# The row exchange of the rotary turns in the second network's query projections: as SBUF to SBUF transfers instead of as products

## The chip, the cores and the metric

The kernel runs on one core of one Trainium2 chip. The metric is the time of one execution in microseconds (us). Before the change it is 2290.31 us, the median of 3 runs (2289.16 to 2290.59).

A core has five engines that matter here: TensorE (PE in the rows, with its weight loads as PEld), VectorE (DVE), ScalarE (ACT), GpSimd (POOL) and SyncE (SP). Each works through its own instructions in order and waits for others at semaphores. SP and ACT can also issue transfers; these are the rows SPq and ACTq. SBUF is the memory on the chip that all engines read, PSUM (eight banks) is what TensorE writes to.

## The reference

Two networks of two layers run one after the other on 256 tokens of width 1024. The change lies in the second, in its two attention mixers. Layer 0 is latent attention: queries and keys are made from low-rank latents, and one part of every query (64 channels per head) is turned by its position. Layer 1 is windowed attention with 16 query heads of 64 channels, all of them turned. The turn is

```
def apply_rope(x, cos, sin):
    x1, x2 = jnp.split(x, 2, axis=-1)
    c = cos[None, :, None, :].astype(x.dtype)
    s = sin[None, :, None, :].astype(x.dtype)
    return jnp.concatenate([x1 * c - x2 * s, x2 * c + x1 * s], axis=-1)
```

(the first network's; the second's is of the same form). In the kernel channels lie on the partitions, two heads of 64 in 128 rows, and tokens along the rows. So x2 stands 32 rows below x1, and the turned tile is `x * cos2 + swap(x) * sin2`, where swap exchanges rows 0..31 with 32..63 and rows 64..95 with 96..127, and the sign sits in the table sin2. The change is about how swap(x) is made.

## The kernel before

It is written engine by engine, with semaphores by hand. Weights come from HBM through four raw buffers (`sb_raw`, issued by SP). ACT copies each panel to a rounded high part (`high(name, n)`, tile `sb_w_hi`), DVE makes the rest (`low(name, n)`, tile `sb_w_lo`), and each is double-buffered; nearly every product is three passes, high by high, high by low and low by high. TensorE may start on a panel when both parts stand (`panel(name, n)` waits for `raw_free`, which `low` raises). The order in which ACT and DVE make panels, evacuate PSUM and do the attention's own steps is written out.

**Latent attention (about 1055 to 1190 us).** Four pairs of heads, p = 0..3. For a pair TensorE makes seven tiles of 128 x 512 in two alternating banks (`pair_tile`, t = 0..3 keys and values in `pair_keys`, t = 4..6 queries in `pair_queries`), and ACT copies each out (`pair_evac`). Tile t may start when tile t-2 has been copied (`tile_free`). The seventh, t = 6, is `qr`, the part that is turned. Its left half, 128 x 256, is swapped by one plain (not split) product with a permutation matrix, `con("rot")`, in `pair_rot(p)`. DVE then runs `pair_rope(p)`: three operations on 128 x 256 whose result is `qrot`. TensorE's `lat_scores(u)` for the first of the four units of a pair (u = 4p) waits for it. A unit u is scores, softmax (DVE `lat_max`, ACT `lat_exp`, DVE `lat_probs`), transposes on TensorE (`lat_flips`), their copies by ACT (`lat_copy`, tile `sb_latPT`), and `lat_products`, which waits for these copies. Pair 0's swap stands in `pair_keys(1)`, those of pairs 1, 2, 3 between the scores and the products of units 0, 5 and 9. Next to them on ACT is, after the copy of t = 6, the high part of the next pair's query panel (`sb_w_hi` 128 x 1536), then the two copies of the unit's transposes.

**Windowed attention (about 1965 to 2066 us).** Seven panels n: 0..3 queries (two tiles of 128 x 256 each), 4, 5 keys (128 x 512 each, these take the context's tokens too), 6 values. After panel n ACT runs `swa_panel(n)`: it copies the bank to `sq_q` (or `sq_k`, `sq_v`) and makes the high part of panel n+2. TensorE swaps group g = n-2 in `rotate(g)` after panels 2 to 5, two plain products of 128 x 256 each time, and the keys' (`rotate(4)`) inside panel 6. DVE makes the lows of panels 4 and 5 with `swa_rope(0)` and `swa_rope(1)` behind them, `swa_rope(2)`, the low of panel 6, `swa_keys`, the low of `swa_o`, `swa_rope(3)`, and goes on with the first maxima. In the same stretch ACT and DVE bring the context's half of the input (`sb_normed`, `sb_h_hi`, `sb_h_lo`), which panels 4 to 6 need.

The lines of the profile: L567 is every product (`mm`), L1324 and L1450 the transposes, L1498 every ACT operation (`run`), L2271 the low parts, L2776, L2778 and L2779 the three operations of a rope, L3139 and L3142 `lat_max`, L518 the weight transfers. `bank` is PSUM, `sb_consts` holds the permutation, cos2 and sin2, and `sb_mid` is the region in which `qr`, `qrot`, `sq_q` and `sq_qrot` lie.

## Time and profile before

| | |
|---|---|
| runs | 2290.31 us median (2289.16 to 2290.59) |
| profiled execution, its own time | 2288.82 us |
| its span in the trace | 2287.0 us |
| PE busy | 2267.6 us, 99% |
| DVE busy | 1697.3 us, 74% |
| ACT busy | 950.1 us, 42% |
| POOL busy | 122.9 us, 5% |
| transfers | 355.08 MB, 44.4% of the 16 DMA engines' time for SP's queue |
| granted TensorE clock | 0.999 of full speed (2.4 GHz) |

The span is what the trace covers; the execution's own time is 1.8 us longer, and this execution is 1.5 us below the median. Busy shares are averages over very different stages. TensorE's matmuls overlap, so the cadence of their starts tells what one costs, not the duration beside it.

### The profile page before, as it was taken

Reading aid. Unit: us, or ns where it says so; the run is one execution under the profiler, and the core shown is the slowest. Engines: PE = TensorE matmul, PEld = TensorE weight load, DVE = VectorE, ACT = ScalarE, POOL = GpSimd, SP = SyncE. Lnnn points to the kernel's source line nnn. Section 1 sums busy time; section 2 is a strip of 40 time slices with the busy share of each in tenths; the row PEclk is TensorE's granted clock in tenths of the full one; section 3 lists DMA queues with packets and bytes.
Section 4 is the critical chain, followed back from the end, with each engine's and each line's share of the span. In section 5 each row is a group of like instructions: output and inputs, shape, how many; then the busy total and the mean of one; then the engine's idle time right before and its main releaser. Section 6 shows DMA issues by size and latency. Waiting matters only on the chain.

```text
span 2287.0 us, 35250 instructions
## 1 busy us (share of the span) xinstructions
PE 2267.6 (99%) x14406; PEld 2014.3 (88%) x14406; DVE 1697.3 (74%) x2772; ACT 950.1 (42%) x1414; POOL 122.9 (5%) x85
## 2 busy tenths in 40 slices
PE   9999999999999999999999999999999999999998
PEld 9899999899998888898789888888888888989997
DVE  7989889989889858754546983884884673797775
ACT  6766645766542122235553212223321222475443
POOL 0110010200100000010001000001000001001001
PEclk9999999999999999999999999999999999999999
DMA  7355475355545545532111553553454453304543
GB/s 281 132 193 187 163 253 193 123 191 192 193 147 208 182 147 187 183 111 83 43 69 56 204 197 105 184 180 115 157 193 157 138 180 102 135 37 148 184 154 124
DMA packets 67025, 355.08 MB, mean 155 GB/s; under 512 B 7344, under 2 KB 10544, under 8 KB 43056
## 3 DMA queue, kind: packets, MB, share of 16 engines
q1 hardware_dynamic: 66304, 352.49, 44.4%
q8 instruction: 114, 1.87, 0.3%
q10 hardware_dynamic: 560, 0.33, 0.0%
q14 instruction: 47, 0.39, 0.0%
HBM read 351.75 MB, written 1.05 MB: 154 GB/s over the span
## 4 chain that ended last, share of the span: by engine, by line
PE 91%; DVE 6%; ACT 2%; issue 0%; DMA 0%; DVEq 0%; ACTq 0%
PE bank L567 90%; DVE sb_w_lo L2271 2%; ACT sb_w_hi L1498 1%; PE bank L1450 1%; DVE sb_products L2305 1%; PE bank L1324 0%; ACT sb_nP L1498 0%; DVE sb_products_up L2323 0%; DMA sb_res<-x 0%; DVE sb_decays L3014 0%; DVE sb_mid L2912 0%; ACT sb_decays L1498 0%; DVE sb_nP L3002 0%; DVE sb_mid L2883 0%; DVE sb_latP L3139 0%
## 5 line engine op out<-in xcount | busy, mean ns | idle before, releaser
L1498 ACT ACTIVATE sb_w_hi<-sb_raw 128x2048 fp32r<-128x2048 f32 (+5 forms) x301 | 491.3, 1634 | 395.6 <-PE bank L567 388.7
L2271 DVE TENSOR_TENSOR sb_w_lo<-sb_raw,sb_w_hi 128x2048 fp32r<-128x2048 f32 (+3 forms) x280 | 563.9, 2014 | 117.5 <-ACT sb_w_hi L1498 112.7
L567 PE MATMUL bank<-sb_f_pair,sb_w_hi 128*128 128x256 f32 (+1 forms) x2090 | 522.6, 339 | 1.5 <-DVE sb_w_lo L2271 1.2
L567 PE MATMUL bank<-sb_h_hi,sb_w_hi 128*128 128x512 f32 (+1 forms) x1400 | 510.8, 365 | 0.6 <-DVE sb_w_lo L2271 0.4
L567 PE MATMUL bank<-sb_h_lo,sb_w_hi 128*128 128x512 f32 (+1 forms) x1400 | 507.3, 362 | 0.0
L567 PE MATMUL bank<-sb_h_hi,sb_w_lo 128*128 128x512 f32 (+1 forms) x1400 | 507.2, 362 | 0.0
L567 PEld LDWEIGHTS bank<-sb_f_pair,sb_w_hi 128*128 128x128 f32 x2090 | 360.2, 190 | 46.5 <-DVE sb_w_lo L2271 3.5
L2305 DVE CUSTOM_DVE_ANT_0 sb_products<-sb_raw,sb_cond,sb_params 128x1024 f32<-128x1024 f32 x276 | 354.8, 1285 | 32.1 <-DVEq L2307 16.2
L567 PE MATMUL bank<-sb_f_pair,sb_w_lo 128*128 128x256 f32 (+1 forms) x1122 | 365.9, 326 | 0.0
L567 PEld LDWEIGHTS bank<-sb_h_hi,sb_w_hi 128*128 128x128 f32 x1400 | 264.1, 189 | 43.0 <-issue 0.9
L567 PEld LDWEIGHTS bank<-sb_h_lo,sb_w_hi 128*128 128x128 f32 x1400 | 264.2, 189 | 41.2 <-issue 0.5
L567 PEld LDWEIGHTS bank<-sb_h_hi,sb_w_lo 128*128 128x128 f32 x1400 | 264.1, 189 | 40.9
L1498 ACT ACTIVATE sb_sil<-bank 128x512 f32<-128x512 f32 x66 | 39.5, 599 | 530.4 <-PE bank L567 530.4
L567 PE MATMUL bank<-sb_raw_hi,sb_w_hi 128*128 128x256 f32 (+1 forms) x910 | 257.0, 282 | 1.9 <-DVE sb_w_lo L2271 1.9
L567 PE MATMUL bank<-sb_raw_hi,sb_w_lo 128*128 128x256 f32 (+1 forms) x910 | 257.1, 283 | 0.0
L567 PE MATMUL bank<-sb_raw_lo,sb_w_hi 128*128 128x256 f32 (+1 forms) x910 | 256.5, 282 | 0.0
L567 PEld LDWEIGHTS bank<-sb_f_pair,sb_w_lo 128*128 128x128 f32 x1122 | 212.8, 190 | 18.0
L552 POOL TENSOR_TENSOR sb_sq_sum<-sb_sq,sb_sq_sum 128x256 f32<-128x256 f32 (+1 forms) x68 | 113.8, 1674 | 2128.9 <-ACT sb_sq L1498 2128.3
L567 PEld LDWEIGHTS bank<-sb_raw_hi,sb_w_hi 128*128 128x128 f32 x910 | 172.4, 189 | 2.6 <-DVE sb_w_lo L2271 2.4
L567 PEld LDWEIGHTS bank<-sb_raw_lo,sb_w_hi 128*128 128x128 f32 x910 | 172.2, 189 | 0.1
L567 PEld LDWEIGHTS bank<-sb_raw_hi,sb_w_lo 128*128 128x128 f32 x910 | 171.7, 189 | 0.0
L2488 DVE SCALAR_TENSOR_TENSOR sb_res<-bank,sb_modT,sb_res 128x256 f32<-128x256 f32 x112 | 49.7, 479 | 164.0 <-PE bank L567 162.8
(330 smaller groups left out, 2926.9 us busy)
## 6 DMA issues: line engine op xcount, KB each, us to landing
sb_raw<-w_mod SPq DMA_DIRECT2D x144, 512.0 KB, 3.2
sb_raw<-w_l_up SPq DMA_DIRECT2D x44, 1024.0 KB, 4.8
sb_raw<-w_l_in SPq DMA_DIRECT2D x22, 1024.0 KB, 6.8
sb_raw<-w_l_down SPq DMA_DIRECT2D x32, 704.0 KB, 4.7
sb_raw<-w_m0a_up SPq DMA_DIRECT2D x22, 1024.0 KB, 4.8
sb_raw<-w_m0b_up SPq DMA_DIRECT2D x22, 1024.0 KB, 4.8
sb_raw<-w_m1a_up SPq DMA_DIRECT2D x22, 1024.0 KB, 4.8
sb_raw<-w_m1b_up SPq DMA_DIRECT2D x22, 1024.0 KB, 4.8
```

Of the source, the lines that this page charges most:

```text
L552: nc.gpsimd.tensor_tensor(sq_sum[:, a:b], sq[:, k % 2, a:b], sq_sum[:, a:b], ALU.add).then_inc(S("sq_added"), 1)
L567: return nc.tensor.matmul(out, lhsT, rhs, start=start, stop=stop, skip_group_check=True)
L1450: last = nc.tensor.transpose(bank[4 + h2][:, c * P:(c + 1) * P], swP[:, u % 2, h2, c * P:(c + 1) * P], ident)
L1498: return nc.scalar.activation(out, in_, func, **kw)
L2271: V.tensor_tensor(split_part(*at, w_lo[s]), landed_part(*at, raw[raw_slot(*at)]), split_part(*at, w_hi[s]).bitcast(F32), ALU.subtract).the ...
L2305: link(V.tensor_tensor_reduce(products[:, :], raw[slot][:, 0:DM], cond[:, s, :], 1.0, par("mod_b", g, g + 1), ALU.mult, ALU.add, modT[:, g ...
L2488: last = V.scalar_tensor_tensor(res[:, k, at:at + T], src[:, at:at + T], mod(l, c, k, s), res[:, k, at:at + T], ALU.mult, ALU.add)
```

## The change

For the queries of both attentions swap(x) is no longer a product into PSUM. After ACT has copied a tile out of PSUM it waits for its own copy, then issues four transfers of 32 rows each, from the tile into the place where the turned tile will stand: 32 x 256 floats (32 KB) for a pair, 32 x 512 (64 KB) for a query group. DVE's rope waits for the four, reads swap(x) from there and overwrites it. TensorE loses four products of `pair_rot` and eight of `rotate(0..3)`; those of the key tile in latent attention and of the keys in the window stay. The waits of TensorE on earlier ropes that guarded the PSUM banks go as well.

```
+        def swapped_rows(queue, out, x, sem):
+            for to in range(4):
+                a, b = slice(32 * to, 32 * to + 32), slice(32 * (to ^ 1), 32 * (to ^ 1) + 32)
+                queue.dma_start(out(a), x(b)).then_inc(S(sem), 16)

 # TensorE
-                if p >= 2 and t == 1:
-                    pe.wait_ge(S("pair_rope"), p)
...
-                    if p == 1 and t == 0:
-                        pair_rot(0)
...
-            def pair_rot(p):
-                _, qr, _, _, _ = pairs[p % 2]
-                pe.wait_ge(S("pair_evac"), 7 * p + 7)
-                mm(rot_bank(p)[:, 0:T], con("rot"), qr[:, 0:T], True, True).then_inc(S("pair_rot"), 1)
...
-                if u in (0, 5, 9):
-                    pair_rot(u // 4 + 1)
...
-                if 2 <= n <= 5:
-                    pe.wait_ge(S("swa_evac"), n - 1)
-                    rotate(n - 2)

 # ScalarE
                     run(dst[t], src, ACT.Copy).then_inc(S("pair_evac"), 1)
                     if t == 3 and p < 3:
                         high(f"mla_pair{p + 1}", 1)
+                    if t == 6:
+                        act.wait_ge(S("pair_evac"), 7 * p + 7)
+                        swapped_rows(act, lambda rows: pair_turned(p)[rows, :], lambda rows: qr[rows, 0:T], f"pair_swapped{p % 2}")
                     if t == 6 and p < 3:
                         high(f"mla_pair{p + 1}", 0)
...
                 last.then_inc(S("swa_evac"), 1)
+                if n < 4:
+                    act.wait_ge(S("swa_evac"), n + 1)
+                    swapped_rows(act, lambda rows: sq_qrot[rows, 2 * n:2 * n + 2, :],
+                                 lambda rows: sq_q[rows, 2 * n:2 * n + 2, :], f"swa_swapped{n}")
                 if n < 6:
                     high(*(("swa_qkv", n + 2) if n < 5 else ("swa_o", 0)))

 # VectorE
-                dve.wait_ge(S("pair_rot"), p + 1)
-                rope(qrot.unsqueeze(1), qr[:, 0:T].unsqueeze(1), rot_bank(p)[:, 0:T].unsqueeze(1), con("cos2"),
+                dve.wait_ge(S(f"pair_swapped{p % 2}"), 64 * (p // 2 + 1))
+                rope(qrot.unsqueeze(1), qr[:, 0:T].unsqueeze(1), qrot.unsqueeze(1), con("cos2"),
                      con("sin2"), 1, "pair_rope", sq)
...
-                dve.wait_ge(S("swa_rot"), g + 1)
+                dve.wait_ge(S(f"swa_swapped{g}"), 64)
```

In the order of instructions this is what stands on ScalarE where pair 2's last tile has been copied, before the change. `sb_mid<-bank` is the copy of `qr`, `sb_w_hi_54` the high part of pair 3's query panel, `sb_latPT` the copies of unit 5's transposes.

```order
L1498 ACTIVATE sb_mid<-bank 128x512 [waits panels_used]
L1498 ACTIVATE sb_w_hi_54<-sb_raw_52 128x1536 [waits landed3,panels_used]
L1498 ACTIVATE sb_latPT<-bank 128x512 [waits lat_flips,lat_prod] x2
L1498 ACTIVATE sb_h_hi<-bank 128x2x128 [waits lat_prod]
L1498 ACTIVATE sb_latP,sb_stat<-sb_latP,sb_stat,sb_q_scale 128x256 [waits lat_max]
```

After the change the same place reads as follows.

```order
L1487 ACTIVATE sb_mid<-bank 128x512 [waits panels_used]
L495 DMA sb_mid<-sb_mid 32x256 [waits pair_evac]
L495 DMA sb_mid<-sb_mid 32x256 x3
L1487 ACTIVATE sb_w_hi_54<-sb_raw_52 128x1536 [waits landed3,panels_used]
L1487 ACTIVATE sb_latPT<-bank 128x512 [waits lat_flips,lat_prod] x2
L1487 ACTIVATE sb_h_hi<-bank 128x2x128 [waits lat_prod]
L1487 ACTIVATE sb_latP,sb_stat<-sb_latP,sb_stat,sb_q_scale 128x256 [waits lat_max]
```

A wait for the copy itself and four transfers now stand ahead of the panel's high part and of the two copies for which TensorE waits.

On TensorE, at the same place (unit 5: transposes, scores of unit 7, swap of pair 2, products), it was:

```order
L1324 MATMUL bank<-sb_consts,sb_latP 128x128 [waits lat_turned,lat_probs]
L1324 MATMUL bank<-sb_consts,sb_latP 128x128 x3
L567 MATMUL bank<-sb_mid 128x256 [waits lat_max]
L567 MATMUL bank<-sb_mid 128x256 x3
L567 MATMUL bank<-sb_mid,sb_consts 128x256 [waits pair_evac]
L567 MATMUL bank<-sb_latPT,sb_mid 128x128 [waits lat_turned,lat_low]
L567 MATMUL bank<-sb_latPT,sb_mid 128x128 x3
```

and it is now:

```order
L1321 MATMUL bank<-sb_consts,sb_latP 128x128 [waits lat_turned,lat_probs]
L1321 MATMUL bank<-sb_consts,sb_latP 128x128 x3
L573 MATMUL bank<-sb_mid 128x256 [waits lat_max]
L573 MATMUL bank<-sb_mid 128x256 x3
L573 MATMUL bank<-sb_latPT,sb_mid 128x128 [waits lat_turned,lat_low]
L573 MATMUL bank<-sb_latPT,sb_mid 128x128 x3
```

The one product with its wait for `pair_evac` is gone; the products of the unit follow the scores at once and still wait for the copies (`lat_turned`).

On ScalarE in the windowed attention, panels 1 to 3 before: `sb_w_hi_54<-sb_raw_52` is the high part of panel 3, `sb_h_hi` the context's input, `sb_w_hi_53<-sb_raw_49` the high part of panel 4.

```order
L1498 ACTIVATE sb_mid<-bank 128x512 [waits panels_used]
L1498 ACTIVATE sb_w_hi_54<-sb_raw_52 128x2048 [waits landed3,panels_used]
L1498 ACTIVATE sb_h_hi<-sb_normed,sb_modT 128x256 [waits norm_scaled] x8
L1498 ACTIVATE sb_mid<-bank 128x512 [waits panels_used]
L1498 ACTIVATE sb_w_hi_53<-sb_raw_49 128x2x8x64 [waits landed0,panels_used]
L1498 ACTIVATE sb_mid<-bank 128x512 [waits panels_used]
```

After:

```order
L1487 ACTIVATE sb_mid<-bank 128x512 [waits panels_used]
L495 DMA sb_mid<-sb_mid 32x512 [waits swa_evac]
L495 DMA sb_mid<-sb_mid 32x512 x3
L1487 ACTIVATE sb_w_hi_54<-sb_raw_52 128x2048 [waits landed3,panels_used]
L1487 ACTIVATE sb_h_hi<-sb_normed,sb_modT 128x256 [waits norm_scaled] x8
L1487 ACTIVATE sb_mid<-bank 128x512 [waits panels_used]
L495 DMA sb_mid<-sb_mid 32x512 [waits swa_evac]
L495 DMA sb_mid<-sb_mid 32x512 x3
L1487 ACTIVATE sb_w_hi_53<-sb_raw_49 128x2x8x64 [waits landed0,panels_used]
L1487 ACTIVATE sb_mid<-bank 128x512 [waits panels_used]
```

Each of the four query copies is now followed by the same block of four transfers, ahead of the high part of the panel after the next.

## Rows read from the trace of the kernel before

**Rows 1.** Page, part 1: busy us (share), instructions.

```profile
PE 2267.6 (99%) x14406; PEld 2014.3 (88%) x14406; DVE 1697.3 (74%) x2772; ACT 950.1 (42%) x1414; POOL 122.9 (5%) x85
```

**Rows 2.** Chain in order of time, 1964 to 2020: start, us, what.

```profile
1963.98 52.80 PE bank L567 x369
```

**Rows 3.** Timeline of PE around `rotate(1)`: start us, us, what.

```profile
1987.34 1.02 PE L567 MATMUL bank<-sb_mid,sb_consts 128*128 128x256 f32 x4
...
1988.43 0.40 PE L567 MATMUL bank<-sb_h_lo,sb_w_hi 128*128 128x512 f32 x1
1988.67 0.39 PE L567 MATMUL bank<-sb_h_hi,sb_w_lo 128*128 128x512 f32 x1
```

**Rows 4.** Timeline of PE around the swap of pair 2.

```profile
1131.67 0.70 PE L567 MATMUL bank<-sb_mid,sb_consts 128*128 128x256 f32 x2
1132.21 1.95 PE L567 MATMUL bank<-sb_latPT,sb_mid 128*128 128x128 f32 x16
```

**Rows 5.** Timeline of ACT's queue at the start of the program.

```profile
0.74 0.44 ACTq L2081 DMA_DIRECT2D sb_params<-params  x1
...
1.74 0.52 ACTq L2083 DMA_DIRECT2D sb_consts<-consts  x1
2.28 1.28 ACT L1498 ACT_TABLE_LOAD   x1 [2.28 <-issue]
```

**Rows 6.** SP's issues of `sb_raw` and `out`: ns min/median/max.

```profile
L518 SPq DMA_DIRECT2D sb_raw<-w_mod x144: 327/328/432, 113.1 to 1853.3; - x144
...
L522 SPq DMA_DIRECT2D out<-sb_normed x4: 372/382/399, 2281.7 to 2284.0; - x4
```

**Rows 7.** Transfers by issue: KB each, median us from issue to landing.

```profile
out<-sb_normed SPq DMA_DIRECT2D x4, 256.0 KB, 2.6
...
sb_params<-params ACTq DMA_DIRECT2D x1, 4.0 KB, 3.4
```

**Rows 8.** Timeline of ACT, copies behind the `qr` tiles of pairs 0, 2, 3.

```profile
1074.61 0.59 ACT L1498 ACTIVATE sb_mid<-bank 128x512 f32<-128x512 f32 x1
...
1131.27 1.08 ACT L1498 ACTIVATE sb_latPT<-bank 128x512 f32<-128x512 f32 x2
...
1162.16 1.09 ACT L1498 ACTIVATE sb_latPT<-bank 128x512 f32<-128x512 f32 x2
```

**Rows 9.** Timeline of PE, what waits for those copies.

```profile
1075.72 0.28 PE L567 MATMUL bank<-sb_w_hi,sb_lat_hi 128*128 128x256 f32 x1
...
1164.47 1.95 PE L567 MATMUL bank<-sb_latPT,sb_mid 128*128 128x128 f32 x16
1166.25 0.60 PE L1324 MATMUL bank<-sb_consts,sb_latP 128*128 128x128 f32 x4
```

**Rows 10.** Timeline of DVE, first operation of pair 3's rope.

```profile
1165.33 0.41 DVE L2776 TENSOR_TENSOR sb_sq<-bank,sb_consts 128x256 f32<-128x256 f32 x1
```

**Rows 11.** Timeline of ACT in the windowed attention, panels 1 and 2.

```profile
1975.67 1.90 ACT L1498 ACTIVATE sb_w_hi<-sb_raw 128x2048 fp32r<-128x2048 f32 x1
...
1984.70 0.58 ACT L1498 ACTIVATE sb_mid<-bank 128x512 f32<-128x512 f32 x1
```

**Rows 12.** Timeline of DVE, lows of panels 2, 3, 4, `swa_rope(2)`, low of panel 6.

```profile
1971.78 2.29 DVE L2271 TENSOR_TENSOR sb_w_lo<-sb_raw,sb_w_hi 128x2048 fp32r<-128x2048 f32 x1 [1.57 <-ACT sb_w_hi L1498]
...
1978.40 2.28 DVE L2271 TENSOR_TENSOR sb_w_lo<-sb_raw,sb_w_hi 128x2048 fp32r<-128x2048 f32 x1
...
1986.26 1.23 DVE L2271 TENSOR_TENSOR sb_w_lo<-sb_raw,sb_w_hi 128x1024 fp32r<-128x1024 f32 x1 [0.82 <-ACT sb_w_hi L1498]
...
1994.81 0.69 DVE L2776 TENSOR_TENSOR sb_swr<-bank,sb_consts 128x512 f32<-128x512 f32 x1 [0.96 <-PE bank L567]
...
1996.99 2.29 DVE L2271 TENSOR_TENSOR sb_w_lo<-sb_raw,sb_w_hi 128x2048 fp32r<-128x2048 f32 x1
```

**Rows 13.** Timeline of PE, `rotate(0)` and `rotate(3)`.

```profile
1980.73 1.02 PE L567 MATMUL bank<-sb_mid,sb_consts 128*128 128x256 f32 x4
...
2000.03 1.03 PE L567 MATMUL bank<-sb_mid,sb_consts 128*128 128x256 f32 x4
```

More of the change, by code:

```diff
@@ L418, in pair_bank, with pair_turned @@
             return bank[2 + (7 * p + t) % 2]
-        def rot_bank(p):
-            return pair_bank(p, 6) if p else bank[5]
+        def pair_turned(p):
+            return pairs[p % 2][2]
         def lat_unit(u):
@@ L1370, in _, with rotate_keys @@
             ready = stream_input((0, 1))
-            def rotate(g):
-                if g >= 2:
-                    pe.wait_ge(S("swa_rope"), g - 1)
+            def rotate_keys():
                 for t in range(2):
-                    turn = mm(bank[4 + g % 2][:, t * T:(t + 1) * T], con("rot"),
-                              sq_q[:, 2 * g + t, :] if g < 4 else sq_k[:, 2 * t, 0:T], True, True)
+                    turn = mm(bank[4][:, t * T:(t + 1) * T], con("rot"), sq_k[:, 2 * t, 0:T], True, True)
                 turn.then_inc(S("swa_rot"), 1)
@@ L1434, in _ @@
                                     pe.wait_ge(S("swa_evac"), 6)
-                                    rotate(4)
+                                    rotate_keys()
                                 last = mm3(bank[6 + t][:, tb * T:(tb + 1) * T],
@@ L3196, in swa_rope @@
             def swa_rope(g):
-                dve.wait_ge(S("swa_rot"), g + 1)
-                rot = bank[4 + g % 2][:, :].rearrange("p (a t) -> p a t", a=2)
-                rope(sq_qrot[:, 2 * g:2 * g + 2, :], sq_q[:, 2 * g:2 * g + 2, :], rot, con("cos2"), con("sin2"), 2,
-                     "swa_rope", swr)
+                dve.wait_ge(S(f"swa_swapped{g}"), 64)
+                turned = sq_qrot[:, 2 * g:2 * g + 2, :]
+                rope(turned, sq_q[:, 2 * g:2 * g + 2, :], turned, con("cos2"), con("sin2"), 2, "swa_rope", swr)
             def swa_keys():
@@ L3208, in swa_keys @@
                 V.tensor_copy(swapped[high_rows, :, T:2 * T], plain[low_rows, :, T:2 * T])
-                dve.wait_ge(S("swa_rot"), 5)
+                dve.wait_ge(S("swa_rot"), 1)
                 rot = bank[4][:, :].rearrange("p (a t) -> p a t", a=2)
```

## The prediction, made before the changed kernel had run

> **What bounds the kernel now.** I read the page's busy shares first, then the chain in order of time in the two stretches that the change touches, then the timelines of each engine there. TensorE is busy 2267.6 of 2287.0 us and ACT only 950.1 [rows 1]. Through the windowed projections the chain is one unbroken piece on TensorE, 52.80 us with 369 matmuls [rows 2]. So a microsecond taken from TensorE is a microsecond off the end, and one in which it waits is added, since nothing later in the program has slack in which TensorE could catch up. ACT's 42% is an average: what counts is what stands behind the new instructions in ACT's order, and how soon TensorE asks for it.
>
> **What goes.** `rotate(1)` starts at 1987.34 and the second wide matmul behind it at 1988.43, 1.09 later; one wide matmul of that, at the ordinary cadence (1988.43 to 1988.67), is 0.24, so the two plain products cost some 0.86 us [rows 3]. Four such groups are 3.4 us. A pair's single product costs 0.54 (1131.67 to 1132.21 [rows 4]), four are 2.2. TensorE is relieved of 5.6 us in all. If nothing else happened the median would fall to 2284.7.
>
> **What comes on ACT.** Each of eight copies is followed by a wait for itself and four issues. The wait: a copy lasts 0.59 but two of them together 1.08 [rows 8], so some 0.1 us of overlap is lost. The issues: no row shows an SBUF to SBUF one. ACT's own at the program's start last 0.44 and 0.52 [rows 5], and while SP issues at the same time; SP's alone last 0.328 (144 of them) and, with more rows, 0.382 [rows 6]. The bounds are 0.33 and 0.55 with the gap between two. I take 0.40, near the 0.382 row plus a gap of 0.02. A block is D = 0.1 + 4 x 0.40 = 1.7 us in which ACT does nothing else; by the bounds 1.4 to 2.3. (A price below nothing is excluded: ACT loses no work.) Eight blocks are 14 us of an engine that is idle for 1300; but they stand ahead of work that TensorE is about to ask for.
>
> The rows show ACT's issues longer, 0.44 to 0.52, when both queues issue, than SP's alone, 0.328 [rows 5, 6]. The Trainium skill's "Perfetto Trace Analysis", section on the HWDGE instruction's lifecycle, has a lock on a shared descriptor generator inside the profiled time, which would explain that; by it blocks that miss SP's issues cost 1.4 to 1.6, and SP issues seldom in both stretches. The skill's "DMA: Bandwidth & Descriptors", section "Issuing engines are not separate DMA queues", calls the time to initiate a transfer "usually small relative to the DMA itself"; taken as a licence to leave it out, it gives the faster rival below.
>
> **Latent attention.**
> - Pair 0. Behind `qr`'s copy stand the high part of pair 1's query panel and the copy of pair 1's first tile, 1074.61 to 1075.20 [rows 8]. TensorE's third tile of pair 1 needs that copy and starts at 1075.72 [rows 9]. Moved by 1.7, the copy ends at 1076.90: +1.2, and the removed product is already in this (TensorE would be there earlier and waits longer).
> - Pairs 1 and 2. Behind the block stand the next high part and the two `sb_latPT` copies, begun at 1131.27 for pair 2, the first done 0.6 later [rows 8]. The products that wait for it start at 1132.21 [rows 4]. Now it is done at 1131.87 + 1.7 = 1133.57: +1.35. Pair 1 has the same sequence with the same distances, again +1.35.
> - Pair 3 has no panel behind it. Copies at 1162.16 [rows 8], done 1162.76, now 1164.46; the products started at 1164.47 [rows 9]: 0, the removed product only turns into a wait. But the rope is late too. The last of the four transfers is issued at about 1163.5. Landing: 2.6 us for 256 KB and 3.4 for 4 KB in the crowded start [rows 7]; I take 2.2 for 32 KB, an estimate under the 2.6 row for the fewer bytes, bounds 2.0 and 3.4. So 1165.7 against the rope's start at 1165.33 [rows 10]: +0.4, which the scores of unit 12 see, as they follow the four transposes of 1166.25 [rows 9] at once. By the bounds 0.2 to 1.6. For the pairs before, the rope ends ahead of the shifted scores.
>
> Sum +4.3, of which the block makes nearly all: each 0.1 of D is 0.3 to 0.4.
>
> **Windowed attention.** Here the ACT blocks push the DVE lows, and TensorE starts a panel when its low stands.
> - Panel 2: low started at 1971.78, lasts 2.29 [rows 12]; with block 0 ahead it ends at 1975.8. Panel 2 ends where `rotate(0)` starts, 1980.73 [rows 13], and its 48 matmuls of 0.12 take 5.75, so it began at 1974.98: +0.8.
> - Panel 3: its high started at 1975.67 [rows 11] and moves by 1.7, its low from 1978.40 [rows 12] to 1980.10, ending 1982.4. Before, panel 3 began at 1980.73 + 0.86 = 1981.6: +0.8 in place of a saving.
> - Panel 4: ACT had no idle time between the context's inputs and the copy of panel 2 at 1984.70 [rows 11], so the delay of the inputs by an earlier block and block 2 both stand ahead of its high: its low moves from 1986.26 [rows 12] by 3.4 to 1989.66, ending 1990.9. Before, the panel began at 1987.34 + 0.86 = 1988.2 [rows 3]: +2.7. This is the largest single wait, 2.7 us between panels 3 and 4.
> - Panels 5 and 6: `rotate(2)` and `rotate(3)` (the latter at 2000.03 [rows 13]) are gone, so TensorE wins back 1.7. DVE from the low of panel 4 to the end of panel 6's low took 1986.26 to 1999.28 with 0.96 of waiting for a product [rows 12], which goes: 12.06 of work, now from 1989.66 to 2001.7. TensorE, at 1990.9 + 2 x 5.48, is there at 2001.9; before it was there at 2000.03 + 0.86 = 2000.9. Net +1.0, and DVE's later chain (keys, last rope, first maxima) is shifted by the same 1.0, so nothing more is lost. Block 3 lies in idle time. The query swaps have 4 us or more to land.
>
> Sum for the stretch +1.0: 3.4 saved, 4.4 waited. Each 0.1 of D counts double here.
>
> **The sum.** +4.3 + 1.0 = +5.3 us. The profiled execution's 2288.82 would become 2294.1; the median of the runs stands 1.5 higher, so 2290.31 + 5.3 = 2295.6. By the bounds: D = 1.4 takes off 0.3 x 5.4 = 1.6 (+3.7), D = 2.3 adds 0.6 x 6 (+8.9), a landing of 3.4 adds 1.2 at pair 3 and perhaps 0.5 at pair 2 (+10.6).
>
> **The rivals.** About 0.2%, 4.6 us, is what a measurement of this kernel can tell from no change.
> - The small one: the same mechanism with issues of 0.33 or less and a little more slack than the rows show. Nothing excludes it: a transfer of 32 rows has a quarter of the rows of SP's. It gives +3.7 down to about 0, say 2293, which reads as no change.
> - Faster: the issues do not hold ACT, because a sequencer hands them off. It decides from D: the sum is 0 at D = 1.7 - 5.3 / 5.4 = 0.7, which is 0.15 us per issue, and at D near 0.1 it is the whole saving, 2284.7. For it: nothing in the timeline says that ACT's next work had to wait for an issue's whole duration. Against it: the table load behind ACT's third issue, which waits for no data, starts at 2.28, when 1.74 + 0.52 has passed [rows 5].
> - The heavy one: swaps share the DMA engines with weight transfers of 1 MB and land late, and issues cost 0.55. Then pairs 2 and 3 wait for their ropes: about +10.5, 2300.8. Against it: in the latent stretch few weights are under way.
> - That the change does not do what it says: the products are gone from the order, so there is no such case.
>
> **How the numbers follow.** Forecast case 0.47, the small one 0.33, faster 0.11, heavy 0.09. The forecast case with +3.7 to +8.9 lies mostly above 4.6. Slower 0.56, within 0.2% 0.34, faster 0.10. Range 2288.0 to 2300.0: it takes in the forecast case, the small one and part of the heavy one, and leaves out the whole saving. The forecast's own range is 2294.0 to 2299.2.
>
> **What would show it.** In the profile of the changed kernel: ACTq rows in blocks of four, 0.33 to 0.45 each; an idle time of PE of about 2 us (1.35 and the missing product) before the products of units 0 and 5, ended by the `sb_latPT` copy; one of about 1.7 us before the third tile of pair 1; about 0.8 us before panels 2 and 3 and 2.7 before panel 4, ended by the low. The forecast is wrong if PE shows no such idle time or if a block lasts under 0.7 us; it is too small if DVE's ropes wait for landings at units 5 and 9.

## The result, and the profile after

The changed kernel takes 2308.43 us, the median of 5 runs (2306.67 to 2312.11), beside 2289.67 us (2289.07 to 2290.59, 5 runs) for the kernel before on the same chip: ratio 1.0082, 95% interval 1.0071 to 1.0093. It is 18.8 us slower. The forecast was 2295.6, 5.3 slower, and its range ended at 2300.0: the sign was right, the size was not. The profiled execution took 2307.52; in the slowest of the five (2312.11) the mean granted clock was 0.994, in the others 0.995 or 0.996.

In the profile of the changed kernel every product is L573, a transpose L1321, every ACT operation L1487, a low part L2267, and L495 issues an exchange. In the other runs these numbers shift by some lines.

The page after, its span and part 1, beside [rows 1]:

```profile
span 2305.7 us, 35229 instructions
PE 2269.7 (98%) x14382; PEld 2015.2 (87%) x14382; DVE 1697.4 (74%) x2772; ACT 950.0 (41%) x1414; POOL 122.8 (5%) x85
```

TensorE lost 24 matmuls, yet was busy 2.1 us longer, in a span 18.7 us longer. Both facts need a reason: the idle time, and matmuls that last longer.

First what ACT does at pair 0, beside [rows 8]. The columns are start, us, engine, line and operation, and in brackets the idle time before.

```profile
1073.39 0.60 ACT L1487 ACTIVATE sb_mid<-bank 128x512 f32<-128x512 f32 x1 [2.12 <-PE bank L573]
1074.02 2.51 ACTq L495 DMA_DIRECT2D sb_mid<-sb_mid  x4
1076.63 1.48 ACT L1487 ACTIVATE sb_w_hi<-sb_raw 128x1536 fp32r<-128x1536 f32 x1 [2.64 <-issue]
1078.02 1.06 ACT L1487 ACTIVATE sb_mid<-bank 128x512 f32<-128x512 f32 x2
```

Copy, four issues, then the high part: between the end of the copy (1073.99) and the high part ACT computes nothing for 2.64 us. That is the block of the prediction, whose length it called D: 2.6 and not 1.7. The issues one by one, and the landings, beside [rows 5 to 7] (ns min/median/max of an issue; KB each and median us to landing):

```profile
L495 ACTq DMA_DIRECT2D sb_mid<-sb_mid x32: 514/612/1500, 1074.0 to 2007.9; - x32
```

```profile
sb_mid<-sb_mid ACTq DMA_DIRECT2D x16, 64.0 KB, 3.5
sb_mid<-sb_mid ACTq DMA_DIRECT2D x16, 32.0 KB, 1.9
```

Then what TensorE waits for, in the latent stretch 1055 to 1215 (the kernel before has no wait there for `sb_latPT` or `sb_mid`; columns: us in total, times, longest) and, below it, in the window from 1985:

```profile
PE bank L573 <- ACT sb_latPT L1487: 7.4, 3, 2.9
PE bank L573 <- ACT sb_mid L1487: 2.6, 1, 2.6
...
PE bank L573 <- DVE sb_w_lo L2267: 6.1, 2, 3.5
```

And the third thing, which the prediction did not have at all: TensorE's clock. The columns are the stretch, its length, PE's busy us and matmuls, the granted clock (1.00 is 2.4 GHz, 0.50 would be 1.2 GHz throughout), DMA share and GB/s.

```profile
1070.00:1076.00 6.00, 6.00 (x27) 1.00 0.44 139
1076.00:1080.00 4.00, 1.42 (x7) 0.77 0.08 21
1080.00:1084.00 4.00, 4.00 (x23) 0.80 0.47 163
1100.00:1104.00 4.00, 1.52 (x7) 0.76 0.06 16
1142.00:1146.00 4.00, 3.06 (x15) 0.63 0.00 0
1175.00:1180.00 5.00, 3.42 (x26) 1.00 0.10 26
2004.00:2008.00 4.00, 1.13 (x3) 0.83 0.37 68
2008.00:2012.00 4.00, 4.00 (x15) 0.75 0.79 293
```

Four times the clock goes to the lower of its two levels for a while: around the waits of 2.58, 2.85 and 2.95 us in the latent stretch and of 3.5 us in the window. It stays full around the one of 1.6 us (1175 to 1180), and around one of 2.60 ahead of panel 2 (which begins at 1991.27). What that costs can be read on the matmuls themselves:

```profile
1078.65 0.58 PE L573 MATMUL bank<-sb_w_hi,sb_lat_hi 128*128 128x256 f32 x1 [2.58 <-ACT sb_mid L1487]
1079.03 0.41 PE L573 MATMUL bank<-sb_w_lo,sb_lat_hi 128*128 128x256 f32 x1
1079.24 0.42 PE L573 MATMUL bank<-sb_w_hi,sb_lat_lo 128*128 128x256 f32 x1
...
1081.72 0.28 PE L573 MATMUL bank<-sb_w_hi,sb_lat_lo 128*128 128x256 f32 x1
1081.84 0.28 PE L573 MATMUL bank<-sb_w_hi,sb_lat_hi 128*128 128x256 f32 x1
```

Starts are 0.21 us apart (1079.03 to 1079.24), and 0.12 once the clock is back (1081.72 to 1081.84). Over the 14 matmuls from 1078.65 to 1081.72 that is 3.07 us in place of 1.7, so some 1.4 us on top of the wait.

The sum over both stretches, of the kernel after and then of the kernel before, closes most of the account:

```profile
1055.00:1215.00 160.00, 149.57 (x828) 0.97 0.18 63
1980.00:2090.00 110.00, 103.66 (x889) 0.98 0.27 87
```

```profile
1055.00:1200.00 145.00, 144.55 (x827) 1.00 0.19 66
1965.00:2070.00 105.00, 104.82 (x902) 1.00 0.23 82
```

Idle time: 10.4 us against 0.5 in the latent stretch, 6.3 against 0.2 in the window, together 16.1 more. The missing clock: 0.03 x 160 + 0.02 x 110 = 7.0 us at most, as the mean is given in hundredths and part of the lower level lies inside the waits, where it costs nothing; at 1.4 to 1.6 us a fall on the matmuls themselves it is about 6. Minus the 5.6 of products: 16.5 to 17.5 of the 18.7. The last 1 to 2 us are not broken down. Part of them is the slow start behind each of the six waits: at pair 0 the second matmul comes 0.38 us after the first, and the next ones 0.21 apart.

### The profile page after: what moved, and what is told of

Same layout as the page of the kernel before. It is cut to its first block, busy times and chain, and to the rows that moved or that the text cites. A ratio compares the mean times of both kernels' runs of the same rounds, so it can differ in the third digit from the quotient of the medians.

```text
span 2305.7 us, 35229 instructions
## 1 busy us (share of the span) xinstructions
PE 2269.7 (98%) x14382; PEld 2015.2 (87%) x14382; DVE 1697.4 (74%) x2772; ACT 950.0 (41%) x1414; POOL 122.8 (5%) x85
## 3 DMA queue, kind: packets, MB, share of 16 engines
q8 instruction: 114, 1.87, 0.3%
## 4 chain that ended last, share of the span: by engine, by line
PE 89%; DVE 6%; ACT 2%; ACTq 1%; issue 1%; DMA 1%; SPq 0%; DVEq 0%
PE bank L573 88%; DVE sb_w_lo L2267 2%; ACT sb_w_hi L1487 1%; ACTq L495 1%; PE bank L1439 1%; DMA sb_params<-params 1%; DVE sb_products L2301 1%; PE bank L1321 0%; DVE sb_mid L2908 0%; ACT sb_mid L1487 0%; DVE sb_products_up L2319 0%; ACT sb_decays L1487 0%; DVE sb_nP L2998 0%; DVE sb_mid L2879 0%; ACT sb_nP L1487 0%
## 5 line engine op out<-in xcount | busy, mean ns | idle before, releaser
L1487 ACT ACTIVATE sb_w_hi<-sb_raw 128x2048 fp32r<-128x2048 f32 (+5 forms) x301 | 491.4, 1635 | 415.7 <-PE bank L573 390.7
L2267 DVE TENSOR_TENSOR sb_w_lo<-sb_raw,sb_w_hi 128x2048 fp32r<-128x2048 f32 (+3 forms) x280 | 563.8, 2014 | 125.7 <-ACT sb_w_hi L1487 121.1
L573 PE MATMUL bank<-sb_f_pair,sb_w_hi 128*128 128x256 f32 (+1 forms) x2090 | 522.6, 339 | 1.5 <-DVE sb_w_lo L2267 1.2
L573 PE MATMUL bank<-sb_h_hi,sb_w_hi 128*128 128x512 f32 (+1 forms) x1400 | 511.4, 365 | 6.8 <-DVE sb_w_lo L2267 6.4
L573 PE MATMUL bank<-sb_h_lo,sb_w_hi 128*128 128x512 f32 (+1 forms) x1400 | 507.9, 363 | 0.0
L573 PE MATMUL bank<-sb_h_hi,sb_w_lo 128*128 128x512 f32 (+1 forms) x1400 | 507.8, 363 | 0.0
L573 PEld LDWEIGHTS bank<-sb_f_pair,sb_w_hi 128*128 128x128 f32 x2090 | 360.3, 190 | 46.4 <-DVE sb_w_lo L2267 3.5
L573 PE MATMUL bank<-sb_f_pair,sb_w_lo 128*128 128x256 f32 (+1 forms) x1122 | 366.0, 326 | 0.0
L573 PEld LDWEIGHTS bank<-sb_h_hi,sb_w_hi 128*128 128x128 f32 x1400 | 264.5, 189 | 49.9 <-DVE sb_w_lo L2267 7.4
L573 PEld LDWEIGHTS bank<-sb_h_lo,sb_w_hi 128*128 128x128 f32 x1400 | 264.6, 189 | 41.1 <-issue 0.5
L573 PEld LDWEIGHTS bank<-sb_h_hi,sb_w_lo 128*128 128x128 f32 x1400 | 264.4, 189 | 41.2
L573 PE MATMUL bank<-sb_raw_hi,sb_w_hi 128*128 128x256 f32 (+1 forms) x910 | 257.1, 283 | 1.9 <-DVE sb_w_lo L2267 1.9
L1487 ACT ACTIVATE sb_sil<-bank 128x512 f32<-128x512 f32 x66 | 39.4, 598 | 530.5 <-PE bank L573 530.5
L573 PE MATMUL bank<-sb_raw_hi,sb_w_lo 128*128 128x256 f32 (+1 forms) x910 | 257.2, 283 | 0.0
L573 PE MATMUL bank<-sb_raw_lo,sb_w_hi 128*128 128x256 f32 (+1 forms) x910 | 256.6, 282 | 0.0
L573 PEld LDWEIGHTS bank<-sb_f_pair,sb_w_lo 128*128 128x128 f32 x1122 | 212.8, 190 | 18.1
L573 PEld LDWEIGHTS bank<-sb_raw_hi,sb_w_hi 128*128 128x128 f32 x910 | 172.4, 189 | 2.6 <-DVE sb_w_lo L2267 2.4
L573 PEld LDWEIGHTS bank<-sb_raw_lo,sb_w_hi 128*128 128x128 f32 x910 | 172.2, 189 | 0.1
L573 PEld LDWEIGHTS bank<-sb_raw_hi,sb_w_lo 128*128 128x128 f32 x910 | 171.7, 189 | 0.0
```

The source lines that it names most:

```text
L573: return nc.tensor.matmul(out, lhsT, rhs, start=start, stop=stop, skip_group_check=True)
L1487: return nc.scalar.activation(out, in_, func, **kw)
L2267: V.tensor_tensor(split_part(*at, w_lo[s]), landed_part(*at, raw[raw_slot(*at)]), split_part(*at, w_hi[s]).bitcast(F32), ALU.subtract).the ...
```

## The experiments

Ten kernels were run. Each has its own runs of the kernel before beside it, and a time with "+" is the difference from their median. In the code "+" and "-" are against the changed kernel, for e7 against the kernel before.

**One half at a time.** e1 leaves the window's products as before, e2 the pairs' products:

```
# e1, PE, window: rotate(g) as before; ACT: no swapped_rows in swa_panel
+                if 2 <= n <= 5:
...
+                    rotate(n - 2)
# e2, PE, latent: pair_rot(p) as before; ACT: no swapped_rows in pair_evac
+                if u in (0, 5, 9):
+                    pair_rot(u // 4 + 1)
```

> Only the latent pairs' swaps are transfers on ScalarE's queue; the window's query groups keep their products. Theory A (each block of four issues holds ScalarE 2.7 us, and each long wait of TensorE behind it also drops the granted clock for some 3 us): the whole shift measured at the end of the latent stretch in the changed kernel, 13.5 us, so about 2303. Theory B (the loss sits in the window, where four more blocks stand ahead of the weight panels): under 6 us, about 2295.

> Only the window's query groups are swapped by transfers; the pairs keep their products. Theory A: the shift gathered between 1965 and 2016 us in the changed kernel, +5.2 us, so about 2295. Theory B: over 12 us, about 2303.

Measured: e1 2302.84 (2301.86 to 2304.33) beside 2290.16, ratio 1.0055 (1.004 to 1.007), +12.7. e2 2296.13 (2295.72 to 2297.01), ratio 1.0026 (1.0016 to 1.0036), +6.0. They add up to 18.7, the whole: no sign that one half changes what the other costs. In e1 TensorE waits for the same things as in the full change, to the tenth: 7.4 and 2.6 us, with the clock at 0.97 in 1055 to 1215. So two thirds of the loss lie in the latent stretch, where the prediction had 4.3, and one third in the window, where it had 1.0. e2's trace has two waits there, 2.44 us ahead of panel 2 and 3.19 ahead of panel 4, each with a fall of the clock: 5.6 us of waiting and some 3 of clock against the 3.4 of products.

**Half of the block off ACT.** e3 gives two of each four transfers to SP's queue, e4 all four. SP issues them at a fixed place between weight transfers.

```
# e3 and e4, SP, ahead of weight panel (name, n)
+                if (name, n) in SWAP_AT:
+                    ...
+                        sp.wait_ge(S("pair_evac"), 7 * g + 7)
+                        swapped_rows(sp, lambda rows: pair_turned(g)[rows, :], lambda rows: qr[rows, 0:T], ...)
...  # the same for the window's groups, behind S("swa_evac")
# e3: ACT issues rows 0..63, SP rows 64..127; e4: ACT issues none
```

> The same transfers, but of each four ScalarE issues two and SyncE the other two, ahead of the weight transfer that next follows. Theory A (the holding time counts, per issue 0.635 us, less the slack that is there once): a block is 1.5 us instead of 2.75; the pairs cost +1.0, +1.1, +1.1 and about 0, the window about +0.5, and no clock drop as the waits are under 2 us: about +4, 2294. Theory C (cost in proportion to the issues): half of +18.7, 2299. Theory D (both queues share one descriptor generator, so two queues issuing at once take turns): ScalarE's issues grow to 1.0 us or more and the time stays near 2305.

> All 32 transfers are issued by SyncE, which waits for the copy and then issues them between two weight transfers; ScalarE issues none. Theory A (what costs is ScalarE's time, not the transfer's): TensorE's waits on ScalarE's copies go; what is left is the landing of 1.9 us or more, which shows at pairs 2 and 3 as about 0.7 us each before the scores of units 8 and 12, and the window wins 2 to 3: about 2288, at least not slower than before. Theory E (the transfer's landing or its share of the DMA engines costs): still over 2298.

e3: 2299.05 (2296.86 to 2299.73), ratio 1.0037 (1.0024 to 1.005), +8.9: theory C's 2299 and not theory A's 2294. e4: 2289.39 (2288.31 to 2289.59), ratio 0.9995 (0.9986 to 1.0004), -0.8: no difference that can be told. TensorE's waits in e3's profiled execution, the fastest of its five (2296.86), latent stretch and window:

```profile
PE bank L587 <- ACT sb_latPT L1501: 4.3, 3, 1.9
PE bank L587 <- ACT sb_mid L1501: 1.6, 1, 1.6
...
PE bank L587 <- DVE sb_w_lo L2281: 3.4, 3, 2.4
```

and in e4:

```profile
PE bank L587 <- DVE sb_mid L2782: 2.1, 3, 1.1
...
PE bank L587 <- DVE sb_w_lo L2274: 0.8, 1, 0.8
```

The waits behind ACT shrink with the number of issues and vanish with the last: the transfers themselves, their landing and the traffic beside them are not what costs 18.7 us; they are the same in e4. e3's waits stayed at 1.93 or less in the latent stretch, and the clock was 1.00 throughout there; around its 2.43 in the window the clock fell once. Theory A had no fall. The two queues also hinder each other, as theory D said, though less than it said: ACT's two issues took 1.49 at pair 0, where SP issued at the same moment, 1.42 at pairs 1 to 3, and 1.16 at best.

e4 also settles whose price the 0.61 us is:

```profile
L495 SPq DMA_DIRECT2D sb_mid<-sb_mid x32: 507/591/1487, 1073.8 to 1992.6; - x32
```

SP needs 0.59 for the same transfer, while its weight transfers (128 rows from HBM, 512 KB) take 0.328 [rows 6]. It is a property of this form, not of ACT. Which part of the form sets it, SBUF at both ends or fewer than 128 rows, was not tried. The longest of these 32, 1.49 us, was issued by SP at 1973.60, while ACT issued nothing: an issue of this length needs no second queue. And in e4 what comes next is shown as well, the ropes of pairs 0, 2 and 3 (`sb_mid` by DVE). The chain at pair 2, start, us, what:

```profile
1129.81 0.61 ACT sb_mid L1501
...
1132.26 1.87 DMA sb_mid<-sb_mid
...
1135.64 3.04 PE bank L587 x12
```

The copy of `qr` ends at 1130.42 and the rope can start at 1134.15, 3.7 us later: four issues (to 1132.26, the last of them in the landing's row) and 1.87 of landing. A product on TensorE takes 0.54. The 2.1 us of waits for these ropes are what the four products of the pairs cost before (2.2).

**Is the clock a cost of its own?** e5 leaves the change as it is and puts four products whose results nobody reads into TensorE's waits at units 0 and 5.

```
+            def filler(p):
...
+                pe.wait_ge(S("pair_evac"), 7 * p + 7)
+                for _ in range(4):
+                    mm(pair_bank(p, 6)[:, 0:T], con("rot"), qr[:, 0:T], True, True)
...
+                if u in (0, 5):
+                    filler(u // 4 + 1)
                 lat_products(u)
```

> The changed kernel, with four 128x128 by 128x256 products, whose results nobody reads, put on TensorE in its order ahead of the products of units 0 and 5, that is, into the two waits of 2.9 us for sb_latPT. The waits themselves stay (about 0.5 us of each, 4 x 0.12, is filled, and ends early in the wait). Theory A: the waits of TensorE are the whole cost, through their own length and through the lower granted clock that follows a long one. A wait that starts 0.5 us later is 2.4 us long; if that is short enough the clock doesn't fall (it fell after 2.6 to 3.5 us, not after 1.6 to 1.9), and the time is 2.8 us less than the changed kernel's, 2305.6. If the fall comes from idle time of 2.4 us as well, nothing changes: 2308.4. Rival B: the fall has nothing to do with the wait, but with the activity around (weights, transfers): then the idle products only cost or cost nothing, 2308.4 to 2309.4, and the clock falls as before.

Measured: 2305.72 (2305.01 to 2307.04, 4 runs). Ratio to before 1.0069 (1.0054 to 1.0085); to the changed kernel, 2.7 us less by the two medians, which are of different batches (the kernel before stood at 2289.67 and 2289.56 in them). The first timeline is of the changed kernel, the second of e5, both at the products of unit 5:

```profile
1142.94 3.65 PE L573 MATMUL bank<-sb_latPT,sb_mid 128*128 128x128 f32 x16 [2.95 <-ACT sb_latPT L1487]
1146.40 0.63 PE L1321 MATMUL bank<-sb_consts,sb_latP 128*128 128x128 f32 x4
```

```profile
1141.31 2.02 PE L573 MATMUL bank<-sb_latPT,sb_mid 128*128 128x128 f32 x16 [1.02 <-ACT sb_latPT L1495]
1143.17 0.60 PE L1327 MATMUL bank<-sb_consts,sb_latP 128*128 128x128 f32 x4
```

The 16 products take 2.02 us in place of 3.65, and by 1143.17 the kernel is 3.2 us ahead of where it was at 1146.40. The eight matmuls of the four products took 1.99 us, and not the 0.5 that the expectation reckoned with, so that of the wait in front only 1.02 us is left idle (0.93 at unit 0). What a wait of 2.4 us does was thus not tried here. The clock in the two places, 0.76 and 0.63 before:

```profile
1100.00:1104.00 4.00, 3.07 (x22) 1.00 0.06 16
1142.00:1146.00 4.00, 3.99 (x24) 1.00 0.01 4
```

At pair 0, which was left without fillers, e5's clock falls as in the changed kernel (0.74 in 1076 to 1080). So the fall follows TensorE's own idle time, it costs some 1.5 us a time, and useless work in the wait removes it. The sizes are less exact, since e5's profiled execution gave 1.7 us of this back in the window. Its panel 2 waited 2.14 us and the clock was at 0.83 in 1985 to 1995, while the changed kernel's execution waited 2.60 there and kept the full clock. Around its wait of 3.23 ahead of panel 4 the clock was at 0.66 in 2000 to 2010, against 0.83 in the changed kernel. The other runs have more such cases: the clock fell around waits of 2.43 (e3) and 2.44 us (e2), and stayed full around one of 2.11 (e9). So between 2.1 and 2.6 us the runs show both, and the length of the wait alone doesn't decide.

**Is the price per issue?** e8 cuts every exchange into eight transfers of 16 rows (DVE waits for all eight).

```
-            for to in range(4):
-                a, b = slice(32 * to, 32 * to + 32), slice(32 * (to ^ 1), 32 * (to ^ 1) + 32)
+            for to in range(8):
+                a, b = slice(16 * to, 16 * to + 16), slice(16 * (to ^ 2), 16 * (to ^ 2) + 16)
```

> The changed kernel, with each exchange cut into eight transfers of 16 rows in place of four of 32, all by ACT: the same bytes and rows, twice the issues. Theory P (the 0.61 us is a price per issue): a block lasts 8 x 0.62 = 5.0 us, TensorE's waits for sb_latPT grow from 2.9 to 5.4, and the time rises by about 2.5 for each pair and some 1.5 to 2.5 for each of four places in the window, 2324 to 2328. Theory R (the price goes by the rows or bytes that a transfer describes): 0.31 an issue, a block of 2.5 us, 2308 to 2310.

One run, so without an interval: 2335.97 us, +46.4.

```profile
L495 ACTq DMA_DIRECT2D sb_mid<-sb_mid x64: 514/611/1823, 1074.1 to 2036.3; - x64
```

```profile
PE bank L573 <- ACT sb_latPT L1487: 15.1, 3, 5.5
```

Half the rows and half the bytes, and the same 0.61: in this form the price is per issue. (In the changed kernel a block of four took 2.44 both at pairs 1 to 3, with 32 KB each, and at panels 1 and 2, with 64 KB.) TensorE's waits for `sb_latPT` are 5.5 at the longest, as 2.9 and one more block of 2.6 would have it. The time rose more than the 2324 to 2328 expected: pair 3's wait, 1.6 before, is 4.1 and now has a fall of the clock with it, there are five waits for `sb_w_lo` in the window, 13.8 us in all, and the clock stays low longer: its mean is 0.57 in the 8 us from 1152, around a wait of 5.5, and was 0.79 in the changed kernel in the 8 us from 1141, around the one of 2.95.

**Where the block stands.** e6 keeps all 32 transfers on ACT and moves each block behind the work that TensorE asks for next. `pair_swap(p)` is the wait for `qr`'s copy and the four issues of pair p.

```
# ACT, latent; pair 0: behind the high part and the first copy of pair 1
                 for h2 in range(2):
                     ...
                     lat_copy(u, h2)
+                if u in (0, 5, 9):
+                    pair_swap(u // 4 + 1)
# ACT, window: swapped_rows after high(n + 2) in place of before it
```

> The changed kernel, all 32 transfers still issued by ACT, but each block moved in ACT's order behind the work that TensorE asks for next: for pair 0 behind the high part of pair 1 and the copy of its first tile, for pairs 1 to 3 behind the two sb_latPT copies of units 0, 5 and 9, in the window behind the high part of the next panel but one. Theory A (what counts is what stands behind the block): the 2.9 us waits for sb_latPT and the 3.5 us waits for sb_w_lo go or shrink below 1 us and the clock does not fall. What comes instead are ropes of pairs 2 and 3 that are late: copy of qr, 1.1 of copies, 2.5 of issues, 1.9 of landing, 5.5 us against the 3.2 from the qr copy to the rope before, so +2.4 each; about 1 at pair 0; window between -2 and +2. In all 2297 (2293 to 2300). Rival B (the transfers themselves, their landing or what they do to the engines, cost the time, wherever they stand): 2306 to 2309. Rival C (nothing waits any more, the saving of 5.6 comes through): 2285 to 2288.

Measured: 2291.53 (2290.73 to 2292.77, 10 runs) beside 2289.56, ratio 1.0008 (0.9999 to 1.0017). That is 17 us less than the change as made, by order alone, and 5 us better than theory A had it. In the two stretches no wait of TensorE is over 1.45 us and the clock doesn't fall. The reason for those 5 us is in ACT's timeline at pair 2:

```profile
1131.19 1.48 ACT L1487 ACTIVATE sb_w_hi<-sb_raw 128x1536 fp32r<-128x1536 f32 x1
1131.66 1.16 ACTq L495 DMA_DIRECT2D sb_mid<-sb_mid  x2
1132.57 0.59 ACT L1487 ACTIVATE sb_latPT<-bank 128x512 f32<-128x512 f32 x1
1132.85 0.61 ACTq L495 DMA_DIRECT2D sb_mid<-sb_mid  x1
1133.05 0.60 ACT L1487 ACTIVATE sb_latPT<-bank 128x512 f32<-128x512 f32 x1
```

The issues stand in the order behind both `sb_latPT` copies, yet the first begins 0.9 us before the first of the copies does. ACT hands out the high part and the copies, and issues transfers while they run. The first three issues lie beside computing, the fourth, at 1133.49, does for its first part. The Trainium skill's "Perfetto Trace Analysis", section "Sequencer Loop", has it so: an engine instruction is only pushed into a queue, and the sequencer reads on. The trace agrees, with the 1131.66 inside the 1131.19 to 1132.67 of the high part.

**Is it the wait for itself?** In the change the block begins with ACT waiting for its own copy of `qr`, the newest piece of work it has handed out, so nothing can be running beside the issues. e9 takes e6's order and adds only such a wait ahead of each block, for ACT's own last piece of work there.

```
+            act.wait_ge(S("pair_evac"), 8)                                   # pair 0
+                    act.wait_ge(S("lat_turned"), 2 * u + 2)                  # pairs 1 to 3
+                    act.wait_ge(S("high"), SPLIT_AT["swa_qkv", n + 2] + 1)   # window
```

> The kernel with the blocks behind the urgent work, in the same order, but each block now first waits for ACT's own latest piece of work to end (the first tile's copy, the second sb_latPT copy, the high part), as in the changed kernel it waited for its own copy. In the run without this wait the issues lay beside running activations (two of pair 2's, 1131.66 to 1132.82, within the high part of 1131.19 to 1132.67; all but the end of a window block beside a high part). Theory S (an issue costs ACT nothing while an activation that was handed out before runs, and the self-wait is what makes it cost its whole 0.61): ACT stands empty for 2.5 us in each block again, ropes of pairs 1 and 2 come 2.1 us later, of pair 3 0.7, of pair 0 1.0, and in the window the copies and high parts behind blocks 0 to 2 come 0.9 to 1.9 later: 2296 (2294 to 2300), with waits of TensorE for ropes (sb_mid) of 3 us and for sb_w_lo of 2 us and more. Theory O (only what stands behind the block in the order counts, the overlap is worth nothing): as without the wait, 2291.5.

Measured: 2299.95 (2299.32 to 2302.93, 5 runs) beside 2290.29, ratio 1.0043 (1.0029 to 1.0057), +9.7; e6 had +2.0. The same place, e9:

```profile
1134.45 1.08 ACT L1487 ACTIVATE sb_latPT<-bank 128x512 f32<-128x512 f32 x2
1135.56 2.44 ACTq L495 DMA_DIRECT2D sb_mid<-sb_mid  x4
```

The issues take 2.44 again, but now ACT computes nothing beside them, and they end 3.55 us after the start of the first copy (1134.45 to 1138.00); in e6 1.53 (1132.57 to 1134.10). TensorE's three waits for the ropes grew from 3.0 us (longest 1.4) to 5.6 (longest 3.1), and behind the 3.1 the clock shows its lower level for a whole stretch:

```profile
1140.00:1146.00 6.00, 5.25 (x12) 0.50 0.01 3
```

Theory S holds, theory O falls. The miss in size (+9.7 against some +5.7 expected) is in good part again the clock, which the expectation had left out: it fell at this place and around a wait of 3.34 us in the window. How much of the median is due to it can't be told, since the profiled execution is the slowest of the five, 2302.93 at a mean clock of 0.996, and three of the others took 2299.3 to 2300.0 at 0.998.

**A version with the transfers only where there is slack.** TensorE waited for no rope of the window in any trace; for those of pairs 0, 2 and 3 it waited even in e4. e7 exchanges only the window's groups by transfers, issued by SP; e10 adds pair 1, whose rope nobody waited for in e4.

```
+        SWAP_AT = {("swa_qkv", 6): 0, ("swa_o", 0): 1, ("swa_o", 1): 2, ("swa_o", 2): 3}
+                if (name, n) in SWAP_AT:
+                    g = SWAP_AT[name, n]
+                    sp.wait_ge(S("swa_evac"), g + 1)
+                    swapped_rows(sp, ..., f"swa_swapped{g}")
```

> The kernel before, with only the window's four groups exchanged by transfers, and these issued by SP's queue between the weight transfers (pairs keep their products). Theory A: 3.4 us of products go; of the waits of the kernel with all 32 by SP only the one of 0.8 for sb_w_lo lies in this stretch, so -2.6: 2287.6. It beats both kernels. Rival B (the products in the window were covered by DVE's lows, which set the pace of the panels): the same as before, 2290.2, with waits for sb_w_lo of 3 us in sum. Rival D (the gain of the SP version lies in the pairs): 2291 or more.

> The kernel with the window's four groups exchanged by SP's queue (2287.6), and pair 1's product also replaced by four transfers from SP's queue, since in the run with all 32 by SP the scores never waited for pair 1's rope. Theory A: 0.54 us less than 2287.6, 2287.1, and no wait of TensorE for a rope. Rival: SP's four issues, 2.4 us ahead of the output panel's weights, or the landing of the exchange beside them, cost as much: 2287.6 or more. The difference of the two is near what can be told apart; what is to be told is whether it stays below the kernel before.

e7: 2287.64 (2286.96 to 2288.4, 11 runs) beside 2289.56 (21 runs), ratio 0.9991 (0.9982 to 1.0). e10: 2287.68 (2287.24 to 2288.34, 11 runs) beside 2290.29 (15 runs), ratio 0.9988 (0.9979 to 0.9997). e10's interval ends just below 1, e7's at 1: a gain of about 2 us, 0.1%, just clear of the noise in e10 and not quite in e7, and no more can be claimed. It is 21 us less than the changed kernel. Pair 1's extra saving can't be told from none. In e7 the one wait of the window is the 0.8 us that e4 has too:

```profile
PE bank L580 <- DVE sb_w_lo L2278: 0.8, 1, 0.8
```

By the trace 2.6 of the 3.4 us of the window's products should come through; 1.9 were measured, which agrees within the noise. It supports the first row of the prediction's sum: a microsecond taken from TensorE there is one off the end.

## Why the prediction was wrong in size

- **The 5.6 us of products** agree with what was measured, as far as it can be told. In the window 3.4 minus a wait of 0.8 leaves 2.6, and e7 measured 1.9 less; with pair 1's 0.54 it would be 3.1, and e10 measured 2.6 less.
- **The block, D = 1.7, bounds 1.4 to 2.3: the first step that failed.** It measured 2.64 us. The issues took 0.61 each, with 0.03 between; I had taken 0.40, near the row of a transfer of 256 KB to HBM, another form. The upper bound, 0.55 from ACT's issues at the program's start [rows 5], was nearer and was also exceeded; I had explained those by SP's traffic. e4 and e8 show that the form sets the price, not the queue, nor 16 or 32 rows. The mechanism was right: with 2.64 in place of 1.7 the prediction's own working for the latent stretch gives waits of 2.7, 2.8, 2.8 and 1.5 us for pairs 0 to 3, and 2.58, 2.85, 2.95 and 1.58 were measured. By the prediction's own slopes (0.3 to 0.4 for the pairs, 0.2 for the window for each 0.1 of D), 0.9 more is +5.0. In the window one issue lasted 1.50 on top (0.9 more). That would have given about +11, still beyond the range.
- **The clock: a term that was missing, the second step that failed.** The sum counted a wait as its own length and put the clock at nothing, without a reason. The granted clock fell around four waits. e5 took away two falls and 2.7 us with them. Four are then 5 to 6 us, an estimate: +11 becomes +17 of the 18.7. It also explains why the loss isn't in proportion to D: e3, with half the issues on ACT, has no fall in the latent stretch.
- **Pair 0, +1.2**: the wait was 2.6, and 1.4 for the clock. **Pairs 1 and 2, +1.35 each** (waits forecast at about 2, the missing product in them): 2.9 each, and 1.4 to 1.6 for the clock. **Pair 3, +0.4**: its wait is 1.6, 7.4 less twice 2.9, and without a fall. The landing was 1.9 where 2.2 was taken, and the rope was never last: TensorE waited for none in the changed kernel, as ACT held the copies longer.
- **Window, +1.0**: measured +6.0 alone. The large wait was where it was forecast, ahead of panel 4 (3.5 us in place of 2.7), behind the two blocks and the context's inputs. Not forecast was the 2.60 ahead of panel 2 (0.8 in the prediction), whose high part stood behind block 0 with the issue of 1.50. The 0.8 forecast ahead of panel 3 did not come, as TensorE was late there already. In the chain:

```profile
1984.73 1.50 ACTq L495
...
1986.98 1.91 ACT sb_w_hi L1487
...
2005.59 1.24 DVE sb_w_lo L2267
2006.87 28.63 PE bank L573 x172
```

- **The rivals.** "Faster: the issues do not hold ACT, because a sequencer hands them off" had 0.11 and the table load of [rows 5] against it. It is half true, and this was worth more than anything else in the case: the issues hold ACT's order, not its running work (e6), and it was the wait for ACT's own copy, which I had priced at 0.1, that made each of them count in full (e9, which adds such a wait, +9.7 against e6's +2.0). "The small one" needed issues of 0.33 or less: excluded. "The heavy one", +10.5, had the nearest issue price (0.55 against 0.61) but the wrong victims, late ropes: none was waited for.
- On the rule of the Trainium skill's "DMA: Bandwidth & Descriptors", "Issuing engines are not separate DMA queues", that initiating is "usually small relative to the DMA itself": here one issue is 0.61 us against a landing of 1.9, a third of it, and the four in a row are 2.4, so for transfers of 32 KB the trace doesn't agree. The lock on the descriptor generator of the Trainium skill's page ("Perfetto Trace Analysis", section "DMA Instruction — HWDGE (DVE, Sync)") would make an issue longer only while both queues issue; SP's 0.59 in e4, where ACT issues nothing, says the base price comes first. The 1.50 in the chain above has SP's last issue 1 us ahead of it, at 1983.77. What made it long is not shown, but e4's 1.49 at 1973.60 came on one queue alone, 1.6 us after the start of a weight transfer's issue, so taking turns between two queues is not needed for it.

## What to carry to other kernels

Price a transfer by its issues as well as by its landing, in the form that will be used, and ask what the issuing engine has running beside them: behind a wait for its own last result they cost their full length, a few instructions later next to nothing. Where an engine at the bound gets new waits, add what the lower clock costs after the long ones; a wait of 2.9 us cost some 4.4 here. Move work off the bound only in places where the replacement's latency has slack: the same exchange from SP's queue left one wait of 0.8 us in the window against 3.4 us of products, and at the pairs waits of 2.1 against 2.2.

## What the runs showed of the hardware

- An SBUF to SBUF transfer of 16 or 32 rows occupies the issuing queue for 0.59 to 0.61 us, on SP and on ACT alike, a weight transfer from HBM for 0.33. Where SP issued at the same moment, two issues of ACT took 1.42 to 1.49 us in place of 1.16 (e3). Single issues of 1.5 us occur, one of them while the other queue issues nothing (e4).
- It lands 1.9 us after its issue in the latent stretch, where little else is under way. In the window, beside weight transfers, it is 3.5 in the median and 6.3 at most (changed kernel).
- TensorE's granted clock went to its lower level around idle times of 2.58, 2.85, 2.95 and 3.46 us in the changed kernel, 2.44 and 3.19 in e2, 2.43 in e3, 2.14 and 3.23 in e5, 3.11 and 3.34 in e9 and 4.1 to 6.0 in e8. It stayed full around 2.60 in the changed kernel, 2.11 in e9 and all those of 1.93 or less. Four idle products, 1.99 us long, in a wait of 2.9 were enough to keep it.
- ACT issues transfers while activations that it handed out earlier are running (two issues, 1131.66 to 1132.82, beside a high part of 1131.19 to 1132.67 in e6).
